# A skewed order of the last two weight units in four output projections and four MLP ends

## What is computed

```
# first block, layer i
x = x + g1 * (concat(mixers(h)) @ w_out[i])            # "output projection"
h = rms_norm(x, norm_ffn[i]) * (1 + sc2) + sh2
x = x + g2 * ((silu(h @ w_gate[i]) * (h @ w_up[i])) @ w_down[i])
# end of the first block: x = rms_norm(x, final_norm)
# second block, layer l: the branch is normed before it is added
x = x + g_m * rms_norm(concat(att, mlstm) @ w_out[l], mix_norm_post[l])
h = rms_norm(x, ffn_norm_pre[l]) * (1 + sc_f) + sh_f
x = x + g_f * rms_norm(swiglu(h, w_gate_up[l], w_down[l]), ffn_norm_post[l])
```

## Time and profile before

| what | value |
|---|---|
| median of 3 runs | 3336.19 us (3333.5 to 3336.36) |
| the profiled execution, whole | 3336.7 us |
| its span, first to last instruction | 3334.9 us |
| TensorE busy | 3192.4 us, 96% of the span |
| VectorE, ScalarE busy | 58%, 34% |
| mean granted TensorE clock | 0.983 |
| TensorE idle in front of L1305, waiting for h_low | 12.8 us in 5 waits |
| warm matmuls (L641) | 142 instructions of 592 ns in the median |

### The profile page before, as it was taken

How to read it: one execution, slowest core, us unless ns; L and a number is a source line. 1 busy time by engine, 2 the same in 40 slices (tenths; PEclk the granted TensorE clock), 3 DMA queues, 4 the chain that set the end, 5 groups by cost and what they waited for, 6 DMA issues and landing times. The chain is left out here.

```text
span 3334.9 us, 44529 instructions
## 1 busy us (share of the span) xinstructions
PE 3192.4 (96%) x17810; PEld 2610.2 (78%) x17810; DVE 1944.6 (58%) x3406; ACT 1135.9 (34%) x2035; POOL 175.6 (5%) x171
## 2 busy tenths in 40 slices
PE   5999999999999999999999999999999999999998
PEld 4988777888888898777877777677877777678886
DVE  4676666746465435667555667756546577643434
ACT  3134644111112424642222434642222535542222
POOL 0000000000000000000000036000000054000000
PEclk8999999999999999999999999999999999999999
DMA  6442113423231221136544231045543221123232
GB/s 213 140 135 80 39 45 97 154 82 114 95 114 58 68 70 51 55 101 208 158 138 149 65 94 59 14 127 190 164 148 117 80 83 45 32 72 99 89 101 76
DMA packets 316030, 335.20 MB, mean 101 GB/s; under 512 B 11896, under 2 KB 219312, under 8 KB 315824
## 3 DMA queue, kind: packets, MB, share of 16 engines
q1 hardware_dynamic: 315824, 332.35, 32.1%
HBM read 328.63 MB, written 3.67 MB: 100 GB/s over the span
## 5 line engine op out<-in xcount | busy, mean ns | idle before, releaser
L2194 DVE TENSOR_TENSOR weights_low<-weights,weights_high 128x1024 fp32r<-128x1024 f32 (+5 forms) x416 | 489.0, 1177 | 765.7 <-ACT weights_high L1535 763.6
L1535 ACT ACTIVATE weights_high<-weights 128x1024 fp32r<-128x1024 f32 (+5 forms) x416 | 420.3, 1012 | 1267.5 <-PE banks L685 799.3
L1305 PE MATMUL banks<-h_high,weights_high 128*128 128x512 f32 (+1 forms) x1760 | 658.6, 374 | 20.0 <-DVE h_low L2206 12.8
L1305 PE MATMUL banks<-h_low,weights_high 128*128 128x512 f32 (+1 forms) x1760 | 651.5, 370 | 0.0
L1305 PE MATMUL banks<-h_high,weights_low 128*128 128x512 f32 (+1 forms) x1760 | 650.9, 370 | 0.0
L685 PE MATMUL banks<-weights_high,h_high 128*128 128x512 f32 (+4 forms) x1360 | 512.0, 376 | 12.8 <-DVE h_low L2206 9.0
L685 PE MATMUL banks<-weights_high,h_low 128*128 128x512 f32 (+4 forms) x1360 | 500.6, 368 | 0.0
L685 PE MATMUL banks<-weights_low,h_high 128*128 128x512 f32 (+4 forms) x1360 | 499.1, 367 | 0.0
L1305 PEld LDWEIGHTS banks<-h_high,weights_high 128*128 128x128 f32 x1760 | 334.0, 190 | 87.3 <-DVE h_low L2206 14.4
L1305 PEld LDWEIGHTS banks<-h_high,weights_low 128*128 128x128 f32 x1760 | 334.1, 190 | 56.6
L1305 PEld LDWEIGHTS banks<-h_low,weights_high 128*128 128x128 f32 x1760 | 334.3, 190 | 52.9
(11 more groups left out here) (406 smaller groups left out, 3793.4 us busy)
## 6 DMA issues: line engine op xcount, KB each, us to landing
projected<-in_w_mod SPq DMA_DIRECT2D x44, 1024.0 KB, 6.3
weights<-in_w_gate_up SPq DMA_DIRECT2D x88, 512.0 KB, 3.8
weights<-in_w_down SPq DMA_DIRECT2D x80, 512.0 KB, 3.8
extra<-in_w_mod SPq DMA_DIRECT2D x36, 1024.0 KB, 6.5
weights<-in_w_in SPq DMA_DIRECT2D x48, 512.0 KB, 3.7
weights<-in_w_gate SPq DMA_DIRECT2D x44, 512.0 KB, 4.6
weights<-in_w_up SPq DMA_DIRECT2D x44, 512.0 KB, 3.9
weights<-in_w_mod SPq DMA_DIRECT2D x32, 512.0 KB, 4.0
```

The lines of the kernel that those rows point to most:

```text
L1305: mm = pe.matmul(bank[:, 0:cnt], wt[:, k, :], x[:, k, a - GOFF:a - GOFF + cnt], start=(k == 0 and q == 0), stop=(k == KD - 1 and q == 2))
L1535: act.activation(WH[s_ % 2][:, 0:k * n], slots[j % LAND][:, 0:k * n], ACT.Copy).then_inc(S["w_high"], 1)
L2194: dve.tensor_tensor(WL[s_ % 2][:, 0:k * n], slots[split_of[s_] % LAND][:, 0:k * n], WH[s_ % 2][:, 0:k * n].bitcast(F32), ALU.subtract).the ...
```

## The change

`product` gets an option `by_tile`, set for the second product of each output projection (`j == 1`) and for the last half of the MLP's last part. The units up to the last two go as before. The last two (unit 0 and unit 1 below) are interleaved: (unit 0, tile 0), (unit 0, tile 1), (unit 1, tile 0), (unit 1, tile 1), and then for each further tile unit 0 and unit 1. The number of warm matmuls falls from 7 to 4 (projections of layers 0 and 1), 11 to 6 (those of 2 and 3), 9 to 6 (end of layer 1) and 11 to 9 (end of layer 2); at the end of layer 0 it stays at 4. The order of the work on ScalarE and VectorE behind an output projection changes with it: the split of the first gate unit moves from ahead of the tiles to near the last tile (layers 0 and 1) or behind all of them (2 and 3), and in layers 2 and 3 ScalarE squares tile i-1 as soon as tile i's own root is taken, while VectorE adds tile i at once instead of one tile later.

```diff
-            def product(..., order=None, by_block=True):
+            def product(..., order=None, by_block=True, by_tile=False):
-                for k, kn in order:
+                for k, kn in order[:-2] if by_tile else order:
...
+                if by_tile:
+                    if ready:
+                        pe.wait_ge(S[low], max(ready[order[-2][1] - 1], ready[order[-1][1] - 1]))
+                    units_there = []
+                    def both(u):
+                        if u == len(units_there):
+                            units_there.append(order[u - 2] + (next_unit(u),))
+                        return units_there[u]
+                    begun = [(0, 0), (0, 1), (1, 0), (1, 1)] + [(u, i) for i in range(2, len(tt)) for u in range(2)]
+                    for u, i in begun:
+                        (k, kn, (wh, wl)), t = both(u), tt[i]
...
+                        if u:
+                            mm.then_inc(B.filled, 1)
+                        elif i == len(tt) - 1:
+                            part_used(mm)
+                    release.append((B.name, B.filled_so_far()))
...
-                warm(7, 6)
+                warm(4, 6)
...
-                warm(11, 4)
+                warm(6, 4)
...
-                    product(GH, GL, OUT_T, (m0, GOFF), 512, m0, m1, lambda i: "d", ready)
+                    product(GH, GL, OUT_T, (m0, GOFF), 512, m0, m1, lambda i: "d", ready, by_tile=(half, m1) == (1, KF))
...
-                warm(11 if second else 4 if with_ctx else 9)
+                warm(9 if second else 4 if with_ctx else 6)
...
 ScalarE, mixed_out
-                for _ in range(3):
+                while nsplit[0] < out_splits:
                     split()
                 for i, t in enumerate(OUT_T):
                     if second:
                         product_squares(1, i)
                         act.activation(R_POST ...)
+                        if i:
+                            whole_squares(i - 1)
                     else:
+                        if t == OUT_T[-1]:
+                            split()
                         residual_squares(1, i, t)
...
                 if second:
-                    for i, t in enumerate(OUT_T): (square the whole tile, root)
+                    whole_squares(len(OUT_T) - 1)
                     for i, t in enumerate(OUT_T):
                         if normed_by[i] == "a":
                             normed_tile(i, t)
+                    split()
                 split()
...
 VectorE, mixed_out
-                for _ in range(4):
+                while nsplit[0] < out_splits:
                     split()
                 for i, t in enumerate(OUT_T):
                     if second:
                         weighed_tile(1, i)
-                        if i:
-                            added_tile(i - 1)
+                        if i == 2:
+                            normed_tile(0, OUT_T[0])
+                        added_tile(i)
...
                 if second:
-                    normed_tile(0, OUT_T[0])
-                    added_tile(last)
                     for i in range(1, last):
                         normed_tile(i, OUT_T[i])
+                else:
+                    split()
                 normed_tile(last, OUT_T[last])
+                if second:
+                    split()
```

21 lines of the change are left out of this document (14 added, 7 removed).

## The result

The changed kernel takes 3311.39 us (median of 4 runs, 3306.22 to 3316.31) where the kernel before takes 3334.88 (4 runs, 3333.5 to 3336.36). The ratio is 0.9931, 95% interval 0.9919 to 0.9944: 23.0 us faster (18.7 to 27.0). Four more executions of the unaltered changed kernel had a median of 3307.01 and a ratio of 0.9922 (0.9909 to 0.9936), 26 us. The forecast was 3318.0 with a range of 3312 to 3326, so the direction was right, and the gain was larger than the range allows, by 0.6 us in the first comparison and by 5 in the second. The forecast gain of 18.7 us lies at the very edge of the first interval and outside the second (21.3 to 30.3).

A forecast was written before the change was run, and what follows sets the result against it. VectorE's and ScalarE's backlog was taken to bound eight places behind projections and MLP ends, up to where warm matmuls become the path. Terms sum to 18.7 us, from 3336.7 to 3318 us, range 3312 to 3326.

The forecast's parts named there:

- the price of the last two units: At all eight places, the last unit is needed after 2.72 us, its low part ready at 2.58: 0.1 us taken.
- layer 0, projection: Behind layer 0's output projection, VectorE no longer late for the last tile, transposes start at 517.95 instead of 521.65: 3.7 us.
- layer 1, projection: Behind layer 1's output projection, three fewer warm matmuls and a chain shortened about as much: 2.5 us gained.
- end of layer 1: TensorE's warm matmuls held the barrier; three fewer, with VectorE's chain 2.1 us earlier and below them: 2.5 us gained.
- layer 2, projection: Behind layer 2's output projection, h_high starts at 19.05 instead of 21.94, ScalarE's queue the new bound: 2.9 us gained.
- end of layer 2: Two fewer warm matmuls; VectorE's chain moves by 2.7 us and then waits for TensorE: 1.6 us gained.
- layer 3, projection: Behind layer 3's output projection, h_high starts at 19.05 instead of 21.94, ScalarE's queue the new bound: 2.9 us gained.
- (2): Rival: ScalarE's queue worse than counted; layers 2 and 3 give 1 us each, first two 1 less: 3324 us, chance 0.12.
- (3): Rival: something else sets the next stage, only the ends of layers 1 and 3 gain: about 3332 us, chance 0.05.
- (4): Rival: the last unit comes late at all eight places, up to 2.55 us each: 3337.6 us, chance 0.04.
- (1): Rival: longer idle behind layers 2 and 3 and elsewhere brings low-clock stretches: 3321.4 to 3325 us, chance 0.14.
- the term of the clock: Behind the projections: up to 3.4 us lost in layers 2 and 3, up to 1.7 won in layer 0, taken as zero.

The follow-up runs named there:

- after_again: The changed kernel once more, unaltered, for a second profile and four more executions: median 3307.01 us, ratio 0.9922 to the kernel before.
- order_only: The changed kernel with its skewed order and moved splits, but the old numbers of warm matmuls: ratio 0.9992 to the kernel before, 2.7 us faster.
- warm_only: The kernel before with only the change's fewer warm matmuls, old order kept: ratio 1.0006 to the kernel before, no gain.
- mixers_only: The change at the four output projections alone, MLP ends and their warm matmuls as before: ratio 0.9954 to the kernel before, 15.3 us faster.
- one_tile_ahead: The changed kernel with the last two units alternating from the first tile, one tile of head start instead of two: ratio 0.9964 to the kernel before.
- no_warm: The changed kernel without warm matmuls at all seven places: ratio 0.9947, 17.7 us faster than the kernel before.
- before_filled_first: The kernel before with 3 warm matmuls added ahead of layer 0's first gate and up product: ratio 0.9984 to the kernel before, 5.3 us faster.
- first_warm_5: The changed kernel with 5 instead of 4 warm matmuls behind layer 0's projection; executed once, only its profile counts: layer 0's MLP stretch 578.89 us.
- mlp_only: The change at the four MLP ends alone, projections, their warm matmuls and queues as before: ratio 0.9974 to the kernel before, 8.7 us faster.

## Why the prediction was right and where it failed

**The terms.** Each gap can be read from some profile at like clock before and after (at the end of layer 0 both are at low clock), and they came out as forecast, and a little better. The forecast's terms hold the price of the last two units, 0.1 us in most; the gaps don't, so it has a row of its own.

| place | forecast | gap before, after | measured |
|---|---|---|---|
| layer 0, projection | 3.7 | 12.04, 8.07 | 4.0 |
| end of layer 0 | -0.1 | 11.63, 11.63 (after_again) | 0.0 |
| layer 1, projection | 2.5 | 10.10, 7.53 | 2.6 |
| end of layer 1 | 2.5 | 14.25 (order_only), 11.68 | 2.6 |
| layer 2, projection | 2.9 | 13.54, 10.28 | 3.3 |
| end of layer 2 | 1.6 | to ScalarE's first work 11.10, 9.37 | 1.7 |
| layer 3, projection | 2.9 | 13.54, 10.28 | 3.3 |
| end of layer 3 | 2.7 | 12.28, 9.56 | 2.7 |
| longer last two units, all eight | (in the terms) | 16.32, 16.37 and 10.88, 10.91 to 10.95 | -0.4 |
| sum (of unrounded terms) | 18.7 | | 19.7 |

The 1.0 us come from three places. The last unit cost 0.03 to 0.07 us a place and not 0.1. In layers 2 and 3 L1568 starts at 7.82 and not at 8.2, 0.3 to 0.4 better each: VectorE adds tile 3 at 13.15 us after the start of the stretch instead of 13.3, and the two splits take 1.99 us in a row. In layer 0 the last tile's transposes came when they were forecast, and `h_high` follows their start by 0.59 us instead of 0.80 (520.01 to 520.60, before 521.65 to 522.45), because ScalarE's split no longer ends behind them. That TensorE's warm matmuls hold the gap, once the tiles are early, is shown by order_only: 10.10 in layer 1, 13.54 in layers 2 and 3 and 16.34 at the end of layer 2 stay as they were. That the backlog holds it otherwise is shown by warm_only in layer 0 (12.26 against 12.04); in layers 2 and 3 the clock is mixed in. That each alone gives little was not said in the prediction, but follows from it.

**The rivals.** (2), ScalarE's queue worse than counted, was wrong: it is the bound, as forecast, and 0.3 to 0.4 us earlier. (3), the gap doesn't matter, was wrong: mixers_only gave 15.3 us. (4), the last unit late everywhere, was wrong by 0.14 us of lead, and one_tile_ahead shows what it would have looked like. (1), the clock takes part of it back, saw longer low stretches behind layers 2 and 3, and there are none: layer 2 keeps its one and layer 3 lost its own. Low clock takes something back at one place that (1) didn't name, the end of layer 2 (1.35 us in both profiles of the changed kernel), and over the whole the rival has the wrong sign.

**The step that failed** is the term of the clock: "I take zero for the sum." I had looked at the low-clock stretches right behind the projections, had bounded a gain by 1.7 us in layer 0 and a loss by 3.4 in layers 2 and 3, and had no term at all for the stretches in the middle of the MLPs. In the profiles two such stretches moved by 5.5 and 3.1 us. The prediction had named just this as what would make it wrong ("a stretch elsewhere, which the change doesn't touch, moves by more than 2 us"). Over all executions the part beyond the gaps is smaller than in the pair of profiles: the two ratios of the changed kernel give 24.5 us, give or take 3, and less the 19.7 of the places that leaves 4.8 us, between 2 and 8. That it is the clock's is read from the profiles; the executions without one agree as far as they can. Over 58 executions of the kernel before, time falls by about 1.0 us per 0.001 of mean granted clock, and the eight of the changed kernel have 0.989 in the mean against 0.986, which by this slope makes 2.8 us (an estimate).

The miss in absolute time has a third part that is no mechanism. The forecast started from the profiled execution of the kernel before, 3336.7 us, and the kernel before then had a median of 3334.88. So the 6.6 us between 3318.0 and 3311.39 are 1.8 of the starting point, 1.0 of the places and 3.8 beyond both, which fall to the clock's term and to the 4 us by which this comparison is uncertain. With the later median as its start, the range (then 3310 to 3324) would just have held the first comparison and still not the second. It took in no gain from the clock beyond layer 0's 1.7 us, and from 3318 it should have reached to about 3305 on the low side.

The Trainium skill (TensorE: Matmul & The Clock Gate, HAM oscillation — how this bites in real kernels) has idle gaps in the stream as what lowers the clock. The traces agree with that where filler is taken away (warm_only, no_warm: slower transposes behind 3.2 us of idle) and where it is added to the kernel before (9.0 and 5.3 us faster). As the prediction read the rule, every longer gap another low stretch, the changed kernel would have lost in layers 2 and 3, where its idle grew from 2.19 to 2.68; it did not.

**What stays open.** That the low clock in layer 0's MLP follows from the idle ahead of it was the first theory. before_filled_first speaks for it (5.3 us, 2.0 to 8.3); first_warm_5 speaks against it as the only cause, since the same idle stood ahead and the stretch was 578.89, and so does mlp_only, with the idle of the kernel before and 576.13. What is shown is that one and the same wait can be followed by low clock or not, in kernels that differ by one warm matmul. A shift alone needn't change it either: after_again reached the stretch 2.6 us earlier than the first profile of the changed kernel and had the same pattern. Single profiles of the shifted kernels can't tell a cause from chance. Whether the changed kernel's 4.8 us are due to its shorter idle, to where its waits happen to fall, or in part to chance among the eight executions is not settled.

## What to carry to other kernels

Where a consumer lags behind TensorE only because all banks fill in the last unit, interleave the last two units by tile, and keep as many tiles of head start as the last unit's preparation takes: here 2.72 us of work over 2.58 us of preparation cost 0.05 us a place, and 1.36 cost 1.4. Then shorten the filler to the new backlog, since filler that outlasts the chain is the path itself; take neither step without the other, and don't take the filler out altogether. When a gain of well under a per cent is forecast on TensorE, give the clock a term with a width of its own, here about 5 us on either side, also for stretches whose work stays the same. And start the forecast from the median of many executions of the kernel before, not from one.

## What the runs showed that I had not expected

Fifty-eight executions of the kernel before lay between 3326.5 and 3340.6 us. Ordered by mean granted clock, those at 0.990 took 3328.5 in the mean (3 executions), at 0.989 3330.6 (3), at 0.988 3332.5 (13), at 0.987 3334.5 (7), at 0.986 3332.4 (10), at 0.985 3334.2 (5), at 0.984 3334.6 (10), at 0.983 3338.1 (6) and at 0.982 3340.6 (1). The spread goes with the clock in part: the correlation is -0.62, so the clock's mean accounts for some four tenths of it. Layer 0's MLP stretch, the same matmuls in every kernel here, took 573.3 us in the quickest of sixteen profiles and 579.1 in the slowest, one_tile_ahead left aside. An idle of 2.93 us in front of the same matmul was followed by low clock in the kernel before and in first_warm_5, and not in the changed kernel, twice. And filler that closed the waits at a layer's start was followed, twice and in two layers each, by 10 us at 0.50 in an attention stretch some 190 us after the layer began, which had none in either profile of the changed kernel, and none in the kernel before with the same filler.
